# Two transformer blocks on one core: the MLP's down product with seven block products in half of its pairs, and its up product by column tiles in one bank

## What is computed

```python
D_MODEL, SEQ, D_FF = 1024, 256, 4096
for i in range(2):
    x = x + mixer(i, rms_norm(x, g_mix[i])) @ w_out[i]
    u = rms_norm(x, g_mlp[i])
    x = x + jnp.square(jax.nn.relu(u @ w_ff1[i])) @ w_ff2[i]
```

## Time and profile before

| | us |
|---|---|
| median of 3 runs (797.8 to 798.32) | 798.21 |
| profiled execution, its own time | 798.14 |
| its span | 796.3 |
| TensorE busy | 789.5 |
| VectorE busy | 530.0 |
| ScalarE busy | 425.1 |

### The profile page before, as it was taken

How to read it: one execution, slowest core, us unless ns; L and a number is a source line. 1 busy time by engine, 2 the same in 40 slices (tenths; PEclk the granted TensorE clock), 3 DMA queues, 4 the chain that set the end, 5 groups by cost and what they waited for, 6 DMA issues and landing times.

```text
span 796.3 us, 11076 instructions
## 1 busy us (share of the span) xinstructions
PE 789.5 (99%) x4150; PEld 658.7 (83%) x4150; DVE 530.0 (67%) x709; ACT 425.1 (53%) x615; POOL 106.9 (13%) x136
## 2 busy tenths in 40 slices
PE   8999999999999999999999999999999999999998
PEld 7998977778888778888888888887778888888886
DVE  6657987767676677576655656678766756666561
ACT  6646655654755564464444454548674545534440
POOL 0500300000130410030000000078900000000000
PEclk9999999999999999999999999999999999999999
DMA  9961463447656634546665565461424566656541
GB/s 344 352 201 40 159 198 121 142 156 287 221 196 201 208 106 149 169 158 213 212 208 175 194 207 170 151 212 54 134 79 159 170 215 223 220 178 208 172 144 53
DMA packets 76230, 142.52 MB, mean 179 GB/s; under 512 B 2928, under 2 KB 21504, under 8 KB 76064
## 3 DMA queue, kind: packets, MB, share of 16 engines
q1 hardware_dynamic: 74128, 135.08, 50.9%
q0 software_dynamic: 1776, 6.84, 2.5%
q10 hardware_dynamic: 288, 0.10, 0.0%
HBM read 140.95 MB, written 1.05 MB: 178 GB/s over the span
## 4 chain that ended last, share of the span: by engine, by line
PE 97%; DVE 1%; ACT 1%; DMA 0%; issue 0%; ACTq 0%; DVEq 0%
PE bank L1776 60%; PE bank L2154 15%; PE bank L2160 7%; PE bank L1949 2%; PE bank L2017 2%; PE bank L1864 2%; PE bank L1798 1%; PE bank L1831 1%; PE bank L1917 1%; PE bank L1991 1%; PE bank L2223 1%; PE bank L1790 1%; PE bank L1997 1%; DMA proj<-in_opening 0%; PE bank L2213 0%
## 5 line engine op out<-in xcount | busy, mean ns | idle before, releaser
L1776 PE MATMUL bank<-w_hi,a_both 128*128 128x512 f32 (+2 forms) x720 | 226.3, 384 | 0.1
L1193 DVE TENSOR_TENSOR w_lo<-raw,w_hi 128x2048 fp32r<-128x2048 f32 (+2 forms) x67 | 152.5, 2277 | 63.2 <-ACT w_hi L712 61.5
L1657 DVE TENSOR_TENSOR w_lo<-raw,w_hi 128x2048 fp32r<-128x2048 f32 x48 | 110.0, 2292 | 90.6 <-ACT w_hi L1095 89.6
L2154 PE MATMUL bank<-a_both,w_hi 128*128 128x512 f32 x512 | 163.2, 396 | 0.0
L712 ACT ACTIVATE w_hi<-raw 128x2048 fp32r<-128x2048 f32 (+2 forms) x67 | 125.9, 1879 | 68.0 <-PE bank L1776 31.2
L1776 PEld LDWEIGHTS bank<-w_hi,a_both 128*128 128x128 f32 x720 | 134.6, 188 | 22.0 <-issue 1.7
L1095 ACT ACTIVATE w_hi<-raw 128x2048 fp32r<-128x2048 f32 x48 | 92.0, 1917 | 112.4 <-PE bank L1776 51.0
L1776 PE MATMUL bank<-w_hi,b_hi 128*128 128x512 f32 x376 | 148.6, 395 | 0.1
L1776 PE MATMUL bank<-w_lo,b_hi 128*128 128x512 f32 x376 | 146.5, 390 | 0.0
L1776 PE MATMUL bank<-w_hi,b_lo 128*128 128x512 f32 x376 | 146.5, 389 | 0.0
L1776 PE MATMUL bank<-w_lo,a_both 128*128 128x512 f32 (+2 forms) x360 | 135.9, 378 | 0.0
(11 more groups left out here) (236 smaller groups left out, 820.4 us busy)
## 6 DMA issues: line engine op xcount, KB each, us to landing
raw<-in_w_ff SPq DMA_DIRECT2D x64, 1024.0 KB, 5.1
raw<-in_w_in_moba SPq DMA_DIRECT2D x20, 512.0 KB, 4.5
raw<-in_w_merge SPq DMA_DIRECT2D x8, 1024.0 KB, 5.0
raw<-in_w_out SPq DMA_DIRECT2D x8, 1024.0 KB, 5.1
m<-in_w_in SPq DMA_DIRECT2D x6, 880.0 KB, 9.3
raw<-in_w_mem_kv SPq DMA_DIRECT2D x4, 1024.0 KB, 5.2
raw<-in_w_ple_gate SPq DMA_DIRECT2D x4, 1024.0 KB, 5.1
raw<-in_w_in_pool SPq DMA_DIRECT2D x4, 1024.0 KB, 5.1
```

The costliest lines, as they stand in the source:

```text
L1193: dve.tensor_tensor(w_lo[:, v % RING, 0:n], landing[land_slot(v)][:, 0:n], w_hi[:, v % RING, 0:n].bitcast(F32), ALU.subtract).then_inc(lo_ ...
L1657: dve.tensor_tensor(w_lo[:, (base + c) % RING, :], raw[:, (base + c) % RAW, :], w_hi[:, (base + c) % RING, :].bitcast(F32), ALU.subtract). ...
L1776: ins = pe.matmul(banks[t][:, 0:n], xa[:, kt, ts], wa[:, slot, w], start=first and k == 0 and q == 0, stop=last and k == kts - 1 and q == 2)
L2154: return pe.matmul(b_hid[f][:, :].rearrange("p (q n) -> p q n", q=2), w_hi[:, slot, w], a_both[:, kt], start=kt == 0, stop=kt == KT - 1)
```

## The change

The hidden columns are taken in pairs of row tiles of the down weights (2 x 128 hidden columns, `c` is the chunk and `h` the half of it). A pair times the 256 tokens and the 1024 output columns is a 2 x 2 by 2 x 2 product of blocks. In pairs with h = 1 of chunks 0 to 6, seven in each layer and 14 of the 28 middle pairs, it is made by seven block products of sums (Strassen's scheme in Winograd's form) in place of eight; the other pairs have eight. The last chunk stays as it was.

For a pair with seven, VectorE forms three differences of weight blocks (`differences`: 1024, 512 and 512 wide), four 128-wide sums of hidden tiles (in `hidden_pair`), and two more remainders (`sum_lo`, 1024 and 512 wide); ScalarE rounds the sums (`sum_hi`, 1024 and 512 wide). The products gather in banks 0 to 3 and in 5, 6 and 7, and at the end of the MLP `flush` combines banks 3, 5, 6 and 7 and adds the parts to x; in pairs with eight one 256-wide difference of hidden tiles goes to bank 2.

Since banks 5 to 7 are taken, up goes one column tile of 128 at a time in bank 4 (`up_columns`), woven with halves of the down product: column, half, column, half. ScalarE copies the whole bank (512 wide) to `halves`, VectorE adds the two halves of two tiles at once. Hidden values of each half chunk have their own place in `tok`, `b_hi` and `b_lo`. The weights are laid out on the host in the units' order (`w_ff`), the MLP's units have four landing slots instead of two, and the loops over chunks are written out. `unit_used`, `lo_ready` and the three-ahead preparation are as before.

```diff
+TP = FF - 1
+SUMS = ((), tuple(range(7)))
...
+def in_sums(u):
+    r = mlp_unit(u)
+    return r is not None and 3 <= r < 4 * FF - 2 and r % 2 == 1 and (r - 3) // 4 in SUMS[(r - 3) // 2 % 2]
...
+        halves = memkv[:, 0, :, :]
+        diff_13, diff_2 = prob[:].rearrange("p t n -> p (t n)"), probT[:, 0:CB]
...
+        sum_hi, sum_lo = [sums[:, 0, j, :] for j in range(2)], [sums[:, 1, j, :] for j in range(2)]
...
+            return u % (RAW_IN if u < U_MERGE or mlp_unit(u) is not None else RAW)
...
+                    act.activation(halves[:, f % 2, :], bank[4 + f if n == 0 else 5 if n == 1 and f == 1 else 4], ACT.Copy)\
+                       .then_inc(ff_part, 1)
+                def hidden_hi(n, h):
+                    act.wait_ge(ff_sq, 2 * FF * lay + 2 * n + h + 1)
+                    act.wait_ge(unit_used, base + 2 if n == 0 else base + 4 * (n - 1) + 2 * h + 5)
+                    c = slice(h * D, h * D + tiles_of(base, n, h) * P)
+                    act.activation(tiles_hi[:, c], tok[:, h, 0:c.stop - c.start], ACT.Copy).then_inc(ff_hi, 1)
+                def split_sums(v, between):
...
+                    act.wait_ge(diffs_made, i)
+                    act.wait_ge(unit_used, v - RING + 2)
+                    act.activation(sum_hi[e][:, 0:2 * CB], diff_13, ACT.Copy).then_inc(diffs_hi, 1)
+                    between()
+                    act.activation(w_hi[:, v % RING, :], landing[land_slot(v)], ACT.Copy).then_inc(diffs_hi, 1)
+                    act.activation(sum_hi[e][:, 2 * CB:3 * CB], diff_2, ACT.Copy).then_inc(hi_ready, 1)
...
+                copy_halves(0, 0)
+                copy_halves(0, 1)
+                hidden_hi(0, 0)
+                copy_halves(0, 2)
+                copy_halves(0, 3)
                 unit(base + 1)
-                def chunk(i, peeled):
-                    for r_ in range(4):
...
-                hidden_hi(lay * FF + FF, base + 2, 4)
+                copy_halves(1, 0)
+                hidden_hi(0, 1)
+                down(base + 5)
+                for c in range(TP):
+                    for h in range(2):
+                        copy_halves(c + 1, 2 * h + 1)
+                        if c == TP - 1 and h:
+                            hidden_hi(FF - 1, 1)
+                            act.activation(flush_m1, bank[5], ACT.Copy).then_inc(m1_copied, 1)
+                            unit(base + 4 * FF - LOOK)
+                            continue
+                        unit(base + 6 + 4 * c + 2 * h - LOOK)
+                        hidden_hi(c + 1, h)
+                        nxt = (c + 1, 2) if h == 0 else (c + 2, 0)
+                        down(base + 7 + 4 * c + 2 * h, lambda: copy_halves(*nxt))
...
+                def hidden_pair(n, h):
...
+                    dve.wait_ge(ff_part, 2 * i)
+                    dve.tensor_tensor(two, halves[:, :, 0:S], halves[:, :, S:2 * S], ALU.add).then_inc(ff_sum, 1)
+                    dve.wait_ge(ff_sum, i)
+                    ins = dve.scalar_tensor_tensor(tok[:, h, 0:CB], tok[:, h, 0:CB], 0.0, tok[:, h, 0:CB], ALU.max, ALU.mult)
+                    if n < FF - 1:
+                        link(ins)
+                        if in_sums(base + 3 + 4 * n + 2 * h):
+                            dve.tensor_tensor(tile[4], tile[1], tile[3], ALU.add)
+                            link(dve.tensor_tensor(tile[6], tile[0], tile[1], ALU.subtract))
+                            link(dve.tensor_tensor(tile[5], tile[4], tile[0], ALU.subtract))
+                            ins = dve.tensor_tensor(tile[1], tile[2], tile[5], ALU.subtract)
+                        else:
+                            both = tok[:, h, 0:CB].rearrange("p (f t n) -> p f t n", f=2, t=NT)
+                            ins = dve.tensor_tensor(tok[:, h, CB:CB + S].rearrange("p (f n) -> p f n", f=2),
+                                                    both[:, :, 0, :], both[:, :, 1, :], ALU.subtract)
+                    ins.then_inc(ff_sq, 1)
+                def hidden_lo(n, h):
+                    dve.wait_ge(ff_hi, 2 * FF * lay + 2 * n + h + 1)
+                    c = slice(h * D, h * D + tiles_of(base, n, h) * P)
+                    dve.tensor_tensor(tiles_lo[:, c], tok[:, h, 0:c.stop - c.start], tiles_hi[:, c].bitcast(F32), ALU.subtract)\
                        .then_inc(ff_lo, 1)
+                def differences(v):
+                    if not in_sums(v):
+                        return
+                    w = landing[land_slot(v)]
+                    dve.wait_ge(raw_landed[land_slot(v)], 16 * landed(v))
+                    dve.wait_ge(lo_ready, v - 1)
+                    link(dve.tensor_tensor(diff_13, w[:, 2 * CB:4 * CB], w[:, CB:3 * CB], ALU.subtract))
+                    link(dve.tensor_tensor(diff_2, w[:, 3 * CB:4 * CB], diff_13[:, 0:CB], ALU.subtract))
+                    dve.tensor_tensor(w[:, 2 * CB:3 * CB], w[:, 0:CB], diff_2, ALU.subtract).then_inc(diffs_made, 1)
+                def down(v):
+                    if not in_sums(v):
+                        unit(v - LOOK)
+                        return
...
+                    dve.wait_ge(diffs_hi, 2 * i - 1)
+                    dve.tensor_tensor(sum_lo[e][:, 0:2 * CB], diff_13, sum_hi[e][:, 0:2 * CB].bitcast(F32), ALU.subtract)
+                    dve.wait_ge(diffs_hi, 2 * i)
+                    dve.tensor_tensor(w_lo[:, v % RING, :], landing[land_slot(v)], w_hi[:, v % RING, :].bitcast(F32), ALU.subtract)
+                    dve.wait_ge(hi_ready, v + 1)
+                    dve.tensor_tensor(sum_lo[e][:, 2 * CB:3 * CB], diff_2, sum_hi[e][:, 2 * CB:3 * CB].bitcast(F32), ALU.subtract)\
+                       .then_inc(lo_ready, 1)
+                def flush():
+                    dve.wait_ge(rstd_sq, lay + 1)
+                    dve.wait_ge(m1_copied, lay + 1)
+                    r2 = [stat[:, 3, 5 + 2 * lay, t:t + 1] for t in range(NT)]
+                    link(dve.tensor_tensor(flush_u2, bank[6], flush_m1, ALU.add))
+                    dve.tensor_tensor(flush_w, bank[3], flush_u2, ALU.add)
+                    link(dve.tensor_tensor(flush_u3, bank[7], flush_u2, ALU.add))
+                    dve.tensor_tensor(flush_u2, bank[3], flush_u3, ALU.add).then_inc(last_ready, 1)
+                    dve.wait_ge(last_ready, lay + 1)
+                    for t, c, part in ((0, 0, flush_m1), (0, 1, flush_w), (1, 0, flush_u3), (1, 1, flush_u2)):
+                        xs = x[:, t, c * CB:c * CB + CB]
+                        ins = dve.scalar_tensor_tensor(xs, part, r2[t], xs, ALU.mult, ALU.add)
+                    link(ins)
                 groups(gx, 2, a_hi, a_lo, gain)
                 if lay:
                     unit(U_OUT1 + 3)
-                unit(base)
-                hidden_square(lay * FF + 1)
+                differences(base + 3)
+                down(base + 3)
+                hidden_pair(0, 0)
+                hidden_lo(0, 0)
+                hidden_pair(0, 1)
                 unit(base + 1)
-                def chunk(i, peeled):
-                    for r in range(4):
...
+                differences(base + 5)
+                hidden_lo(0, 1)
+                down(base + 5)
+                for c in range(TP):
+                    for h in range(2):
+                        ahead = base + 7 + 4 * c + 2 * h
+                        if c < TP - 1:
+                            differences(ahead)
+                        hidden_pair(c + 1, h)
+                        if c == TP - 1 and h:
+                            hidden_lo(FF - 1, 1)
+                            flush()
+                            unit(base + 4 * FF - LOOK)
+                            continue
+                        unit(ahead - 1 - LOOK)
+                        hidden_lo(c + 1, h)
+                        down(ahead)
...
+                def products_of(u):
+                    if in_sums(u):
+                        return [(5, 0, 1), (0, 2, 0), (2, 1, 3), (1, 3, 2), (3, 4, 4), (6, 5, 6), (7, 6, 5)]
+                    return [(0, 0, 1), (1, 1, 1), (2, 4, 2), (3, 1, 2), (0, 2, 0), (1, 3, 0), (2, 5, 3), (3, 3, 3)]
...
+                        for ta, wa, sums in ((tiles_hi, w_hi, sum_hi), (tiles_hi, w_lo, sum_lo), (tiles_lo, w_hi, sum_hi)):
+                            for b, i, j in halves_[q]:
+                                at = h * D + i * P
+                                ins = pe.matmul(bank[b], ta[:, at:at + P], piece(wa, sums, j), start=b not in begun,
+                                                stop=ta is tiles_lo and closing.get(b) == (u, i))
+                                begun.add(b)
+                        if q:
+                            ins.then_inc(unit_used, 1)
...
+                for c in range(TP):
+                    for h in range(2):
+                        u = base + 2 + 4 * c + 2 * h
+                        half_of = down_products(u + 1, c, h)
+                        up_columns(u, c, 2 * h)
+                        if c == 0 and h == 0:
```

(16 more changed lines are left out.)

224 lines of the change are left out of this document (108 added, 116 removed).

## The result

The changed kernel takes 806.88 us (median of 4 runs, 806.72 to 807.71), the kernel before 798.27 in the same session: ratio 1.011, 95% interval 1.0092 to 1.0127. It is slower by 8.6 us, where 804.3 was forecast. The profiled execution took 807.71 (span 805.9, 9.6 above the span before), 0.8 more than the other three; the trace is set against that.

What follows compares the result with a forecast made beforehand. TensorE's instruction stream, busy 99% of the span, was taken as the bound. From 798.2 us, 9.5 removed, 9.4 for start waits, 4.8 for layer 0's end and 1.4 for the clock added: 804.3 us, range 798 to 811.

Steps and rivals of the forecast that it cites:

- What is taken out: TensorE's stream: 42 matmuls fewer in 14 pairs, 9.5 us; new up order and four banks put at nothing.
- Rival (c): Down product in four banks: step between matmuls falls from 0.2267 to 0.2133 us, 8.4 us less, 795.9; chance 0.05.
- The steady state: MLP chunks: VectorE needs 19.8 of 21.4 us per two pairs; three-engine chain 12.5 us against 13.1, cost nothing.
- rival (d): MLP chunks: the three-engine chain outgrows its 0.6 us cover, or VectorE is slower, 807 to 813 us; chance 0.18.
- The start of each MLP: First seven-product pair waits 2.9 us for VectorE, then copies cost 0.45 and 1.35; 4.7 per layer, 9.4 for both.
- Rival (b): MLP starts: VectorE reaches the first seven-product pair in time, no start waits, 794.9 us; chance 0.12.
- The end of layer 0: End of layer 0's MLP: additions, updates and two `w_lo` ahead of `add_half` make the transposes of x 4.8 us late.
- The load order, one load of 1 MB for each unit, stays: Weight loads: with four MLP landing slots instead of two, loads only come earlier; cost nothing.
- The clock after that wait: Behind the 4.8 us wait at layer 0's end: granted clock falls to the lower level, costing 1.4 us.
- rival (e): Both MLP starts: the clock falls there as well and stays low for a product, 807 to 811 us; chance 0.12.
- The sum: Whole kernel: 798.2 - 9.5 + 9.4 + 4.8 + 1.4 = 804.3 us.
- (a): Whole kernel: the likeliest case, all terms as summed, 801.5 to 807 us; chance 0.53.

Runs made afterwards that it cites:

- the early ones: Changed kernel, 14 pairs, attention groups ahead of units at MLP end, plus layer 0's first weight differences made early: 802.1 us, ratio 1.0051.
- the best version: Changed kernel with 12 seven-product pairs, groups ahead of units at MLP end, third unit landing in `m`, later landing slots exchanged: 794.95 us, ratio 0.9956.

## Why the prediction was right, and where it was off

- **What is taken out** held: 42 matmuls at 0.227, in the new bank order too. Rival (c), a shorter step, is out: 109 matmuls take 21.43 us, as forecast. The new order, put at nothing, costs 0.5 us in layer 1.
- **The steady state** held: 19.21 us of VectorE against 19.8, no wait in any chunk; rival (d) is out.
- **The start of each MLP** held in mechanism and nearly in size: 28.7 us against 28.7 for the last remainder, waits of 2.6 and 2.45 against 2.9, the smaller ones 0.16 and 1.19 in layer 1 against 0.45 and 1.35. Layer 1 cost 5.1 for 4.7, in part by luck: its three waits were 0.9 shorter than forecast, and the new order and the restarts, which were not in the sum, made up for it. That the pairs with seven products make it, the runs without them and with twelve show; that in layer 0 it is the late differences, the early ones show. Rival (b) is out.
- **The end of layer 0** held: 4.8 late, as summed; `add_half` ended 15.0 us after the last up column and TensorE was there after 10.2, both as forecast. What the step missed is that VectorE's order at this place also releases a landing slot. "The load order, one load of 1 MB for each unit, stays", put at nothing, was the wrong step. The load of the third unit is tied to the first unit's `w_lo`, 12 us later than before. That came out as 1.2 us here, and as 5.4 us as soon as the first wait was taken away.
- **The clock after that wait** was undersized: 2.0 against 1.4. And rival (e) came true by half: in the profiled execution the clock fell at layer 0's start, which cost 3.0 us, and not at layer 1's; the small waits forecast in layer 0 didn't come behind the slower stream (1.8 us less).
- The sum, term by term: start waits 9.4 forecast, 10.9 measured with the clock; end 4.8 and 4.8; clock 1.4 and 2.0; nothing and 1.2. These are terms of the profiled execution, which add up to 3.3 more than forecast; the median was 2.6 above the forecast. What was missing is the clock, and the load behind it. The median, 806.88, lies just under the upper end of (a), 807, where (e) begins.

What stays open: the best version is 5.0 us above 36 matmuls less than before (798.2 - 8.2 = 790.0). 2.1 is its wait for prob, 1.5 the one for x, and a stretch at half clock behind the first, from 538 to 542, costs some 1.7. These are readings of one profiled execution, no run takes them out one by one. Why the two waits remain, whether by the loads or by VectorE's longer list there, the runs don't settle.

## What to carry to other kernels

A stream on the bounding engine gets shorter only by what its helpers can hide at the seams: 42 matmuls, worth 9.5 us in a steady chunk, were lost at three places where a list of short VectorE work met a reader. Before an edit puts work ahead of an operation, ask not only who reads that operation, but which buffer it frees: in a ring of two landing slots a late remainder makes the load two units on late, the load itself takes 4 to 5 us, and the loss comes out in another stage. And when one wait is removed, look for what it covered before counting the gain.
